# Transposes of the odd head ahead of the next pair's scores in a neighbourhood attention

## The reference

```
def even_mixer(h, ...):
    u = h @ w_in0
    q_lat, kv_lat, k_rope, na_q, na_k, na_v, gate = split(u)
    o_mla = mla(q_lat, kv_lat, k_rope, ...)           # 8 heads, every query sees 512 keys
    o_na = neighbourhood_attn(na_q, na_k, na_v, rpb)  # 8 heads of 64 channels
    o = concatenate([o_mla, o_na]) * silu(gate)
    return o @ w_out0

def neighbourhood_attn(q, k, v, rpb):      # tokens are a grid of 8 rows x 64 columns
    ...                                    # a query sees the 8 rows x 16 columns around it
        s = einsum('bchd,bjkhd->bhcjk', q_r, k_r)
        s = where(col_in, s + bias, -inf)
        p = softmax(s)
        return einsum('bhcjk,bjkhd->bchd', p, v_r)
```

## Time and profile before

| | |
|---|---|
| median of 3 runs | 1494.59 us (1493.46 to 1497.82) |
| the profiled execution | 1495.35 us |
| its span | 1493.2 us |
| PE busy | 1454.1 us, 97% |
| DVE, ACT, GpSimd busy | 57%, 46%, 24% |

### The profile page before, as it was taken

How to read it: one execution, slowest core, us unless ns; L and a number is a source line. 1 busy time by engine, 2 the same in 40 slices (tenths; PEclk the granted TensorE clock), 3 DMA queues, 4 the chain that set the end, 5 groups by cost and what they waited for, 6 DMA issues and landing times.

```text
span 1493.2 us, 18901 instructions
## 1 busy us (share of the span) xinstructions
PE 1454.1 (97%) x7162; PEld 1111.9 (74%) x7162; DVE 854.8 (57%) x1523; ACT 679.5 (46%) x1169; POOL 365.7 (24%) x455
## 2 busy tenths in 40 slices
PE   8999999999999999999999999999999999999996
PEld 5677765678777787788888887567877778787885
DVE  7523345665787527885444344575688652788433
ACT  3323446744433435543544344674543353554233
POOL 2021023421200022765210002342120002375311
PEclk9999999999999999999999999999999999999998
DMA  9566832214332331106324533211432333111531
GB/s 385 200 220 213 254 131 86 61 59 136 106 94 83 118 108 57 43 29 240 97 89 161 141 109 117 85 57 58 155 106 85 95 111 106 50 43 45 176 93 68
DMA packets 54618, 174.27 MB, mean 117 GB/s; under 512 B 6000, under 2 KB 7408, under 8 KB 52224
## 3 DMA queue, kind: packets, MB, share of 16 engines
q1 hardware_dynamic: 54528, 173.07, 35.5%
HBM read 149.94 MB, written 23.10 MB: 116 GB/s over the span
## 4 chain that ended last, share of the span: by engine, by line
PE 84%; DVE 8%; ACT 4%; issue 2%; DMA 2%; POOL 1%; SPq 0%; DVEq 0%; ACTq 0%; POOLq 0%
PE ps L561 22%; PE ps L563 21%; PE ps L562 21%; PE ps L1113 3%; PE ps L1149 2%; PE ps L1168 2%; PE ps L1659 1%; PE ps L1642 1%; PE ps L303 1%; DVE w_lo L543 1%; PE ps L1693 1%; PE ps L1482 1%; PE ps L1187 1%; PE ps L1130 1%; DMA at<-z_kept 1%
## 5 line engine op out<-in xcount | busy, mean ns | idle before, releaser
L543 DVE TENSOR_TENSOR w_lo<-at,w_hi 128x1024 fp32r<-128x1024 f32 x160 | 200.0, 1250 | 347.6 <-ACT w_hi L531 347.5
L531 ACT ACTIVATE w_hi<-at 128x1024 fp32r<-128x1024 f32 x162 | 169.4, 1047 | 132.1 <-PE ps L563 124.5
L561 PE MATMUL ps<-h_e_hi,w_hi 128*128 128x512 f32 x464 | 184.3, 397 | 4.0 <-DVE w_lo L543 4.0
L563 PE MATMUL ps<-h_e_hi,w_lo 128*128 128x512 f32 x464 | 180.8, 390 | 0.0
L562 PE MATMUL ps<-h_e_lo,w_hi 128*128 128x512 f32 x464 | 180.6, 389 | 0.0
L561 PE MATMUL ps<-h_a_hi,w_hi 128*128 128x512 f32 x384 | 153.6, 400 | 2.1 <-DVE h_a_lo L593 1.3
L562 PE MATMUL ps<-h_a_lo,w_hi 128*128 128x512 f32 x384 | 149.7, 390 | 0.0
L563 PE MATMUL ps<-h_a_hi,w_lo 128*128 128x512 f32 x384 | 149.6, 389 | 0.0
L561 PEld LDWEIGHTS ps<-h_e_hi,w_hi 128*128 128x128 f32 x464 | 87.1, 188 | 38.2 <-DVE at L1468 10.1
L563 PEld LDWEIGHTS ps<-h_e_hi,w_lo 128*128 128x128 f32 x464 | 87.1, 188 | 18.6
L562 PEld LDWEIGHTS ps<-h_e_lo,w_hi 128*128 128x128 f32 x464 | 87.2, 188 | 17.7 <-issue 0.5
(11 more groups left out here) (292 smaller groups left out, 2996.5 us busy)
## 6 DMA issues: line engine op xcount, KB each, us to landing
at<-blocks_in SPq DMA_DIRECT2D x162, 512.0 KB, 3.7
at<-w_ada SPq DMA_DIRECT2D x32, 512.0 KB, 4.6
at<-w_ada SPq DMA_DIRECT2D x8, 1024.0 KB, 17.9
at<-xs SPq DMA_DIRECT2D x4, 2048.0 KB, 10.4
z_kept<-at SPq DMA_DIRECT2D x32, 256.0 KB, 2.1
at<-z_kept SPq DMA_DIRECT2D x32, 256.0 KB, 2.8
sg_kept<-at SPq DMA_DIRECT2D x16, 256.0 KB, 4.5
at<-sg_kept SPq DMA_DIRECT2D x16, 256.0 KB, 2.7
```

The lines of the kernel that those rows point to most:

```text
L531: act.activation(whi[:, n % PAIRS, :, cols], wring[:, n % SLOTS, :, cols], ACT.Copy).then_inc(sem("w_hi"), 1)
L543: dve.tensor_tensor(wlo[:, n % PAIRS], wring[:, n % SLOTS], whi[:, n % PAIRS].bitcast(F32), ALU.subtract)\
L561: pe.matmul(o, stationary[0], moving[0], start=first, stop=False)
L563: return pe.matmul(o, stationary[1], moving[0], start=False, stop=final)
```

## The change

Inside pass i of PE's loop, the call of `score_quad(i)` moves from ahead of `turn(i - 3)` to behind it. The two projection steps between them belong to passes 25 and 27, in which there are no scores. Passes below 16 and above 23 stay as they were.

```
@@ -1196,13 +1196,13 @@
                     score_pair(i)
                     if i in (0, 2):
                         latent_values(2 + i // 2)
-                elif i < HALVES and i % 2 == 0:
-                    score_quad(i)
                 if i in (HALVES + LT - 2, HALVES + LV - 1):
                     for k in (0, 1) if i < HALVES + LT else (2, 3):
                         out0(pe, 0, k)
                 if LT <= i < HALVES + LT:
                     turn(i - LT)
+                if MLA_END <= i < HALVES and i % 2 == 0:
+                    score_quad(i)
                 if i >= LV and i % 2:
                     values_of_two(i - LV)
```

## The result

The changed kernel takes 1503.35 us (median of 5 runs, 1500.39 to 1506.17), the kernel before 1494.57 beside it. The ratio is 1.006 with a 95% interval of 1.0045 to 1.0074: 8.8 us slower, where 7.9 were forecast.

A forecast was written before the change was run, and what follows sets the result against it. Bound: a 6.41 us ring of scores, DVE maxima, DVE copy, transposes and values in near attention. Moved transposes add 3.96 us a group, 7.9 in two: 1494.59 + 7.9 = 1502.5 us; range 1499.5 to 1505.0.

The forecast's parts named there:

- The ring: Near attention: scores, row maxima, DVE copy, second four transposes of the even head, values set the period of 6.41 us.
- The 0.25 us a period: Allowance in the range's upper end, 1505.0 us, for PE's start behind a long wait, which no row shows.
- The price of a block: Eight transposes moved between values and scores add 0.97 us at each of four score steps, 3.88 us a group.
- The upper bound from the chain: Highest price row for eight transposes in a row, 1.02 us; with it the median would be 1503.0 us.
- The inputs of a moved block: Whether moved transposes find normalised rows and copies ready in near attention: -0.05, +0.10, no wait and +0.03 us.
- turn(15): Odd-head transposes moved ahead of the scores at 283.39; they want ACT's copy, ready at 283.49: +0.10 us.
- turn(19): Transposes moved ahead of the last scores; ACT's copy allows 296.30 at the earliest, the slot is 296.27: +0.03 us.
- turn(13): Transposes moved ahead of the first scores; they hide the scores' 0.05 us wait for an ACT exponential: -0.05 us.
- The sum: Both near attentions: 3.88 - 0.05 + 0.10 + 0.03 = 3.96 us a group, 7.9 us in two groups.
- Rival A: Near attention: DVE's copy comes earlier, PE becomes the bound, 6.7 us faster, 1487.9 us; chance 0.04.
- Rival B: DVE's 0.83 us subtraction hides the cost in two of four pairs: 3.9 us slower, 1498.5 us; chance 0.08.
- Rival C: PE's clock drops to 1.2 GHz for a whole near attention: 47 us more in two groups, 1550; chance 0.02.

The follow-up runs named there:

- E1: Changed kernel, but only the first four of the odd head's eight transposes go ahead of the scores: 1498.62 us, ratio 1.0023 to the kernel before.
- e2: Kernel before with the new order at only one of the four score blocks of each group: 1496.01 us, ratio 1.0010.
- e6: Kernel before in its own order, plus eight transposes of a constant between values and scores at each of four score blocks: 1503.16 us, ratio 1.0053.
- e3: Changed kernel with the first four transposes of each of four even heads issued three times: 1502.35 us, ratio 1.0046 to the kernel before.
- e7: Kernel before with each odd head's second four transposes issued twice, behind the scores: 1493.28 us, ratio 0.9986.
- e4: Changed kernel with DVE's copy of the odd head's transposes ahead of the new scores' maxima in four passes: 1502.43 us, ratio 1.0042 to the kernel before.
- e5: Changed kernel measured again, nothing altered, beside the kernel before on the same chip: 1504.14 us, ratio 1.0063.
- e9: Changed kernel again, unaltered, beside two kernels with repeated transposes filling PE's stands: 1504.52 us, ratio 1.0070 to the kernel before.

## Why the prediction was right

- *The ring.* Scores, maxima, DVE copy, second four transposes, values: each link of the changed trace is within 0.01 us of that before (1.65; 1.47 to the copy; 0.72; 0.58; 1.88). The periods became 7.43 to 7.48 where 7.4 was forecast. The 0.25 us a period that the range kept for PE's start behind a long wait was not needed: the 0.72 is as before.
- *The price of a block.* 0.97 was taken, 1.02, 0.99, 1.02 and 1.00 measured (274.96 to 275.98, 282.46 to 283.45, 289.86 to 290.88, 297.36 to 298.36), 4.03 a group where 3.88 was forecast. The upper bound from the chain was the better row. E1, e2 and e6 showed that it is the place and the number that cost, and e3 and e7 that transposes behind the scores are free as long as PE waits there anyway.
- *The inputs of a moved block.* turn(15) was to be 0.10 late for ACT's copy: the values end in 282.38 (280.50 plus 1.88) and the block starts at 282.46, so 0.08. turn(19) was to be 0.03 late, and is: 1.96 us from the start of the values (295.40) where it was 1.93. turn(13) was to gain 0.05 and gained 0.12: from the values to what follows it is 1.88 us now (273.08 to 274.96) and was 2.00 (275.00 to 277.00). The prediction took the end of the shown duration, 276.95, for the end of the values, though that duration overlaps what follows.
- *The sum.* 3.96 us a group forecast, 3.99 and 4.02 measured. That it fits to 0.03 is in part luck: in the first group the blocks cost 0.15 more than forecast, the inputs came to about nothing where 0.08 was forecast, and the stretches from scores to values were 0.04 shorter than before, mostly behind the fourth score block.
- *Rival A*, faster, failed as said, since DVE's order kept the maxima first; and e4 showed that it would have failed with the copy in front as well, for ACT's copy, which I had not named.
- *Rival B* failed: DVE's idle time before the maxima grew in all four pairs (1.94, 2.50, 1.94 and 1.20 us where it was 1.03, 1.42, 0.91 and 0.21), so PE stayed the later one in the pair with the subtraction too.
- *Rival C*, the clock, was wrong as priced (47 us, for a whole near attention at the lower level) and right in kind. I had read one stand of 1.39 us at full clock as reason enough to leave a fall out. The changed kernel has eight stands of 1.63 to 1.64, and in two of three profiles one of them was followed by a fall of 1.65 us. A granted clock below 1.00 in a near attention is one of the prediction's own signs of being wrong: the first profile doesn't have it, those of e5 and e9 do. The sum left this term at nothing. It may be most of the 0.8, 1.9 and 2.2 us by which the medians (8.8, 9.9, 10.2 above before) lie over the 8.0 of the stretches, but not surely: e6, without long stands, lies 0.9 over as well.

## What to carry to other kernels

When work is moved on the engine that bounds, ask first whether it stood in the shadow of a wait: moved out of it, it costs its full length, though nothing was added and PE's busy time stayed the same (1454.1 us before, 1452.2 in the changed kernel's first profile). Completing an input earlier gives nothing as long as the in-order stream of its reader has something ahead of it that waits for the very thing that was delayed; moving the order of one reader was not enough here, since the next one (ACT's copy) then held the ring, so all readers have to be checked. A stand on PE was filled with work that cost nothing, and filling it may even save clock, which the runs do not settle.

## What the runs showed of the hardware

PE's granted clock fell to its lower level (3-us windows at 0.60 to 0.63) inside a near attention in which PE never stood longer than 1.64 us at once (e5, e9), and once behind a stand of 1.86 us (e4). I had given the clock 2 chances in 100. In such a fall the values took 3.30 us in place of 1.95 (e5) and 3.66 in place of 2.01 (e9); each of these two falls made its group 1.65 us longer. Eight transposes of 128x128 in 4 bytes took 0.97 us (before) and 0.99 to 1.02 us (changed) from start to start, at a granted clock of 1.00.
